# The recurrent mixer's projections spread one to a level over the first attention's last two levels and the second's first six, and the second attention's values behind them

## The reference

```python
p = (u @ w_in).astype(jnp.float32)
p_pool, p_hg, p_rw, p_gla = jnp.split(p, [G, 5 * G, 5 * G + RWKV_COLS], axis=-1)
...
prev = jnp.pad(p_rw, ((0, 0), (1, 0), (0, 0)))[:, :T]
p_rw = p_rw + (prev - p_rw) * rwkv_mu
rr, rk, rv, xw, xa, xg = jnp.split(p_rw, [...], axis=-1)
w_log = -jax.nn.softplus(-(rwkv_w0 + jnp.tanh(xw) @ rwkv_w2)) - 0.5
a = jax.nn.sigmoid(rwkv_a0 + xa @ rwkv_a2)
g_r = jax.nn.sigmoid(xg) @ rwkv_g2
kk = split_heads(rk * rwkv_k_k)
kk = kk / jnp.maximum(jnp.sqrt(jnp.sum(kk * kk, axis=-1, keepdims=True)), 1e-12)
rk = rk * (1.0 + (a - 1.0) * rwkv_k_a)
o_r = rwkv7_scan(r_h, split_heads(decay), k_h, v_h, kk, split_heads(a))
```

## Time and profile before

| | |
|---|---|
| median of 3 runs | 1793.57 us (1792.46 to 1795.89) |
| profiled execution, its own time | 1796.89 us |
| its span, first to last instruction | 1795.1 us |
| mean granted clock of TensorE | 0.969 |
| TensorE busy | 1722.1 us |
| VectorE busy | 875.8 us |
| ScalarE busy | 674.9 us |
| GpSimdE busy | 129.5 us |

### The profile page before, as it was taken

One profiled execution on the slowest core, in us unless ns is written; L12 is line 12 of the kernel. 1 busy time (PEld: TensorE's weight loads), 2 busy tenths in 40 slices (PEclk: granted clock), 3 DMA queues, 4 the chain that ended last, 5 costly groups with the idle time before them and its releaser, 6 DMA issues.

```text
span 1795.1 us, 22262 instructions
## 1 busy us (share of the span) xinstructions
PE 1722.1 (96%) x8752; PEld 1405.7 (78%) x8752; DVE 875.8 (49%) x1169; ACT 674.9 (38%) x1017; POOL 129.5 (7%) x126
## 2 busy tenths in 40 slices
PE   7999999999999899999999999969998899999997
PEld 6777778878778788888888777859986688888886
DVE  5633445532445565444334774665345654444333
ACT  5145664225555333332224443463132433333221
POOL 0001002001001000000004000001330200000000
PEclk9999999999999999999999999965999999999998
DMA  5322213322222133223333211100001222333331
GB/s 188 125 71 71 83 51 103 126 81 75 78 65 83 59 107 103 96 94 89 97 97 141 71 59 48 61 17 1 1 19 47 82 83 95 99 100 92 96 97 56
DMA packets 40744, 143.91 MB, mean 80 GB/s; under 512 B 4816, under 2 KB 4832, under 8 KB 40384
## 3 DMA queue, kind: packets, MB, share of 16 engines
q1 hardware_dynamic: 37008, 130.87, 22.6%
q0 software_dynamic: 2192, 8.73, 1.5%
q10 hardware_dynamic: 1440, 2.88, 0.4%
HBM read 140.37 MB, written 2.10 MB: 79 GB/s over the span
## 4 chain that ended last, share of the span: by engine, by line
PE 79%; DVE 13%; ACT 5%; issue 1%; ACTq 0%; DVEq 0%
PE bank L450 22%; PE bank L452 21%; PE bank L451 21%; PE bank L432 9%; DVE sb_w_low L1115 2%; DVE sb_E L1115 2%; PE bank L438 2%; DVE sb_near L1502 1%; PE bank L668 1%; PE bank L647 1%; ACT sb_E L1833 1%; PE bank L604 1%; ACT sb_w_high L1833 1%; DVE sb_xg_low L1123 1%; DVE sb_x L1115 1%
## 5 line engine op out<-in xcount | busy, mean ns | idle before, releaser
L1115 DVE TENSOR_TENSOR sb_w_low<-sb_raw,sb_w_high 128x1024 fp32r<-128x1024 f32 (+1 forms) x253 | 310.0, 1225 | 391.1 <-ACT sb_w_high L1833 385.2
L450 PE MATMUL bank<-sb_xg_high,sb_w_high 128*128 128x512 f32 x1176 | 469.2, 399 | 26.0 <-DVE sb_xg_low L1123 16.1
L452 PE MATMUL bank<-sb_xg_high,sb_w_low 128*128 128x512 f32 x1176 | 461.9, 393 | 0.0
L451 PE MATMUL bank<-sb_xg_low,sb_w_high 128*128 128x512 f32 x1176 | 461.7, 393 | 0.0
L1833 ACT ACTIVATE sb_w_high<-sb_raw 128x1024 fp32r<-128x1024 f32 (+1 forms) x253 | 263.2, 1040 | 357.1 <-PE bank L452 325.3
L450 PEld LDWEIGHTS bank<-sb_xg_high,sb_w_high 128*128 128x128 f32 x1176 | 223.0, 190 | 93.0 <-issue 33.3
L452 PEld LDWEIGHTS bank<-sb_xg_high,sb_w_low 128*128 128x128 f32 x1176 | 222.9, 190 | 47.8
L451 PEld LDWEIGHTS bank<-sb_xg_low,sb_w_high 128*128 128x128 f32 x1176 | 223.3, 190 | 44.7
L452 PE MATMUL bank<-sb_h_high,sb_w_low 128*128 128x512 f32 x352 | 136.9, 389 | 0.0
L450 PE MATMUL bank<-sb_h_high,sb_w_high 128*128 128x512 f32 x352 | 136.9, 389 | 0.0
L451 PE MATMUL bank<-sb_h_low,sb_w_high 128*128 128x512 f32 x352 | 136.9, 389 | 0.0
(11 more groups left out here) (334 smaller groups left out, 2123.4 us busy)
## 6 DMA issues: line engine op xcount, KB each, us to landing
sb_raw<-w_ffn_in SPq DMA_DIRECT2D x88, 512.0 KB, 3.3
sb_raw<-w_ffn_out SPq DMA_DIRECT2D x32, 512.0 KB, 3.6
sb_raw<-w_tok SPq DMA_DIRECT2D x24, 512.0 KB, 3.7
sb_raw<-w_mix_f SPq DMA_DIRECT2D x18, 512.0 KB, 3.2
sb_raw<-w_rot SPq DMA_DIRECT2D x16, 512.0 KB, 3.7
sb_raw<-w_qk SPq DMA_DIRECT2D x16, 512.0 KB, 3.3
sb_raw<-w_out SPq DMA_DIRECT2D x16, 512.0 KB, 3.2
sb_raw<-w_ffn_out SPq DMA_DIRECT2D x16, 384.0 KB, 3.1
```

Of the source, the lines that this page charges most:

```text
L450: e.matmul(out, w[0], v[0], start=first, stop=False)
L451: e.matmul(out, w[0], v[1], start=False, stop=False)
L452: return e.matmul(out, w[1], v[0], start=False, stop=last)
L1115: e.tensor_tensor(out, a, b, op).then_inc(*v.up(*signal))
```

## The change

The recurrent projections start in the first attention's levels 8 and 9, with the two that feed the decay and the gates (`RWKV_ORDER` begins with 6 and 7), and go on with one in each of the second's levels 0 to 5. The second attention's four value units fill its levels 6 to 9. The operand steps become functions of their own, called from the levels between which their inputs are ready. Several operands get buffers that others leave: projections go straight to `rE`, `kI`, `rv` and `gates_in` in place of `mixed`, the scan's sum and the decay are raised in place (`cum`, `sigma`), and the two gates (`gates_in`) and `shifted` lie where gla's values come later. The first half of the mixing waits for `far` of size 128 alone and for each token tile's values by itself. The SiLU of gla's gate moves from level 4 to the place behind the root in `finish_gla`.

```diff
+
+RWKV_ORDER = (6, 7, 2, 3, 0, 1, 4, 5)
...
     order += [t["w_mix_ga"]] + mixer_tiles(14, 16, 15, 17)
-    values, projections = mixer_group(1), mixer_tiles(*range(2, 10))
-    order += values[0:3] + [projections[0], values[3]] + projections[1:]
+    order += mixer_tiles(*(2 + f for f in RWKV_ORDER)) + mixer_group(1)
...
         r = region(first_at, second_at)
-        m.mixed = r.room("mixed", 8, SEQ)
-        m.shifted = r.room("shifted", 2, SEQ)
+        m.rE, m.kI, m.rv, m.bI = (r.room(n, 2, SEQ) for n in ("rE", "kI", "rv", "bI"))
+        m.sigma = r.room("sigma", 2, SEQ)
+        r = region(values_at, end)
+        m.gates_in, m.shifted = r.room("gates_in", 2, SEQ), r.room("shifted", 2, SEQ)
+        m.own = [room[:, f, :] for room in (m.rE, m.kI, m.rv, m.gates_in) for f in range(2)]
...
                 i = take(("mixed", name, half), ("mixed landed", name, half))
                 p.wait_ge(*of("near done", name))
-                p.wait_ge(*of("far", name, last, 3))
-                p.wait_ge(*of(landed("v", 3), name, 3))
+                p.wait_ge(*of("far", name, last - 1 + half, 3))
                 for t in (2 * half, 2 * half + 1):
+                    p.wait_ge(*of(landed("v", t), name, t))
                     for h in HEADS:
...
         def rwkv_steps():
-            for f in range(8):
+            for f in RWKV_ORDER:
                 projected("rwkv", f, "rwkv landed", f)
                 yield
...
+        projections = rwkv_steps()
+        values_h, others = token_major("v", "hgrn", 1, n), gla_steps()
+
+        def decay_and_gate_in():
...
+        def gate_out():
+            for half in range(2):
+                i = take(("gate out", half), ("g tok", half))
+                p.wait_ge(*of("rwkv sigmoid"))
...
+        def key_norm():
             i = take(("key norm",), ("key floored",))
             p.wait_ge(*of("key squares"))
...
+        def key_turned():
             for f in range(2):
                 i = take(("key turned", f), ("key scaled", f))
                 p.wait_ge(*of("key spread"))
...
+        def bonus_sums():
             i = take(("bonus",), ("bonus",))
             p.wait_ge(*of("rE"))
...
+        def fill_hgrn(n):
+            if n == 0:
+                next(values_h)
+                next(values_h)
+                pool_outputs()
+            else:
+                next(values_h if n < 3 else others if n < 8 else projections)
+            if n == 9:
+                decay_and_gate_in()
+
+        linear_attention("hgrn", fill_hgrn)
+        values_g = token_major("v", "gla", 1, n)
         def fill_gla(n):
-            if n < 2:
-                next(values_g)
-                next(projections)
-            elif n < 6:
-                next(projections)
-                if n in (2, 4):
-                    next(projections)
-                if n == 5:
-                    p.mark("xg read", MIX_NORM)
-            else:
-                next(operand_prep)
+            next(projections if n < 6 else values_g)
+            if n == 1:
+                gate_out()
+            if n == 3:
+                key_norm()
+            if n == 4:
+                key_turned()
+            if n == 9:
+                p.mark("xg read", MIX_NORM)
+                bonus_sums()
...
+            if n == 0:
+                finish_hgrn()
+            if n == 3:
+                key_floor()
+            next(projections if n < 6 else values_g)
+            if n == 1:
+                decay_sums()
+            if n == 5:
+                keys_scaled()
+            if n == 6:
+                keys()
+            if n == 7:
+                receptance()
+            if n == 8:
+                receptance_faded()
...
             fill(len(ORDER))
+            if name == "gla":
+                a.wait_ge(*of("bonus in"))
+                act(small[:, 112:128], bank("bonus")[:, 0:16], "bonus")
             for half in range(2):
...
+        def decay_in():
+            a.wait_ge(*of("rwkv mixed", 6))
+            act(m.gates_in[0:64, 0, :], m.gates_in[0:64, 0, :], "rwkv tanh", func=ACT.Tanh)
...
         def fill_hgrn(n):
+            if n == 9:
+                decay_in()
...
-            yield
+        values_g = value_steps("gla")
+
+        def gates():
+            a.wait_ge(*of("y made", "hgrn"))
...
+            a.wait_ge(*of("rwkv mixed", 7))
+            act(m.gates_in[:, 1, :], m.gates_in[:, 1, :], "rwkv sigmoid", func=ACT.Sigmoid)
+
+        def gate_out():
             for half in range(2):
                 a.wait_ge(*of("gate out", half))
...
-            yield
+
+        def key_squares():
+            a.wait_ge(*of("rwkv mixed", 3))
+            for f in range(2):
...
+        def decay_exps():
             a.wait_ge(*of("sigma before"))
             act(m.eB, m.cum, *STEP, func=ACT.Exp, scale=-HALF_E)
-            act(m.rE, m.cum, *STEP, func=ACT.Exp, scale=HALF_E)
-            act(m.tmp, m.tmp, "rwkv exps", func=ACT.Exp, scale=-HALF_E)
...
+        def key_spread():
+            a.wait_ge(*of("key inverse"))
+            act(heads(flat(mem.square)), small[:, 176:192].unsqueeze(2).to_broadcast([P, 16, 64]), "key spread")
...
+            if n == 0:
+                finish_hgrn()
+                gates()
+            if n == 2:
+                key_squares()
+                decay_exps()
             if n == 4:
-                bend_gate("gla")
+                key_spread()
+            next(projections if n < 6 else values_g)
+            if n == 1:
+                gate_out()
...
-        inverse(m, finish_gla)
+
+        def gla_out():
+            finish_gla()
+            bend_gate("gla")
+
+        inverse(m, gla_out)
```

191 lines of the change are left out of this document (69 added, 122 removed).

## The result

The changed kernel takes 1814.84 us, median of 4 runs (1813.39 to 1815.61), against 1794.32 for the kernel before on the same chip (4 runs, 1792.46 to 1795.89): a ratio of 1.0114, 95% interval 1.0096 to 1.0131. It is **slower by 20.5 us**. The profiled execution has a span of 1811.6 us against 1795.1, so 16.5 us of it can be followed in the two traces. (Four executions further down stand apart from the others of their kernel, at a lower mean clock: 1933.9 us in run 7, 2849.6 in run 12, 1808.4 and 1808.7 in run 10; the medians count them, the ratios do not.)

A forecast was written before the change was run, and what follows sets the result against it. A second-attention level with one projection was taken as bound by VectorE and ScalarE, not TensorE. +15.5 us up to the first product with Pm and +2 in the inverse gave +17.5, on the median 1811 us; 80% range 1794 to 1827.

The forecast's parts named there:

- the first product that reads Pm: Behind the second attention's Gram products, ahead of the inverse: comes at 1268.9 us against 1253.4, 15.5 us later.
- the inverse: Behind a gap of 2 to 3 us its clock may fall: 2 us in the sum, bounds 0 and 75.
- the last value unit: Made behind the second attention's last 256-wide products, ahead of the mixing: 7.4 us, between 5.7 and 11.4.
- VectorE's chain: Serial steps through the second attention's levels: 102.3 us from "y made", last factors ready at 1211.6 us against 1198.9.
- y made: VectorE finishes the first attention's output, where the second attention's chain starts: at 1109.3 us against 1110.1.
- last operand: The last VectorE step that the inverse needs ("rE"), 3.8 us behind the last factors: 1215.4 us against 1221.0.
- TensorE's wait at the turned keys: In filling 4 of the second attention: TensorE ends projection 4 near 1153 us and waits until 1164.5.
- The mixing falls to half after some 2 us and takes 15.5: Second attention's mixing, behind the two-column bonus sums: clock falls to half, from near 1225.5 us to 1241.
- Rival 2: Clock returns with the last value unit and holds through mixing and Gram products: 1796 to 1799 us; 25%.
- The Gram products at half, and the SiLU: From the mixing's end to the first product with Pm: 25.5 us at half clock plus 2.4 for the SiLU.
- rival 1: Half clock in mixing, Gram products and a good part of the inverse: some 1822 us, up to 1840; 22%.
- What follows the inverse is untouched: Stages behind the inverse to the end of the span: no change in time.

The follow-up runs named there:

- run 7: The changed kernel with bonus sums behind the inverse's last pass, early SiLU, early weight splits and projection 5 at level 4: 1796.53 us, ratio 1.0020 to the kernel before.
- run 12: The kernel before with only the loosened end (presets of X, output squares and sums, and root earlier): 1795.58 us, ratio 1.0004.
- run 10: As run 9, and projection 5 made at level 4, so no value unit is left behind the last factors: 1783.35 us, ratio 0.9935 to the kernel before.
- Run 1: The changed kernel with projection 5 one level earlier, at level 4 beside projection 4: 1807.85 us, ratio 1.0082 to the kernel before.
- run 4: The changed kernel with ScalarE's splits of the weight's high part ahead of sigmoids, squares and exponentials: 1814.57 us, ratio 1.0113 to the kernel before.
- run 2: The changed kernel with the two-column bonus sums behind the mixing instead of ahead of it: 1806.45 us, ratio 1.0067 to the kernel before.
- run 11: The changed kernel with only the bonus sums moved, into TensorE's wait ahead of the last 256-wide products: 1802.48 us, ratio 1.0048 to the kernel before.
- run 9: The changed kernel with early weight splits, bonus sums in the wait ahead of the 256-wide products, and presets, SiLU, squares and root earlier: 1783.06 us, ratio 0.9938.
- run 5: The changed kernel with bonus sums behind the inverse's last pass and the SiLU among the token copies: 1802.32 us, ratio 1.0044 to the kernel before.
- run 6: As run 5, with ScalarE's splits of the weight's high part early as well: 1793.24 us, ratio 1.0000 to the kernel before.
- Run 3: The changed kernel with the gate's SiLU among ScalarE's copies of the turned tokens: 1806.88 us, ratio 1.0076 to the kernel before.
- run 8: The kernel before with 24 more unused 128x512 products between its last 256-wide product and the second attention's mixing: 1792.82 us, ratio 0.9990.

## Why the prediction was right, point by point

It said 1811 us, 17.5 us more on the span; measured were 1814.8 and 16.5 on the profiled spans. Median and profiled execution part by the spread between executions: the profiled one was the fastest of its four runs. That the sum on the span came within 1 us is partly luck: the first product that reads Pm came 3.6 us sooner than forecast, and 1.1 us more in the inverse and 1.5 us behind it filled most of that again. The mechanism held; its largest miss is the last value unit.

- **VectorE's chain.** "y made" was said to come at 1109.3 and came at 1107.5; the whole of TensorE's timeline ahead of it is 1.3 us early. The chain of 102.3 us took 101.9, with last factors at 1209.4 (said: 1211.6) and the last operand at 1213.0 (said: 1215.4). Its waits for two weights, 5.1 and 4.8, were 4.99 and 4.85. Run 1 shows that the chain and not TensorE sets this end, run 4 that it moves with those splits. (Before, four of the second's levels carried two units, not three; the sum does not use it.)
- **TensorE's wait at the turned keys**, until 1164.5, ended at 1163.0 behind 9.71 us. Runs 1, 7 and 10 add what I had not priced: filling it lengthens the chain by 2.0 to 3.3 us and makes another wait, for the banks of the values.
- **The last value unit** was put at 7.4 us, between 5.7 and 11.4. It took 5.8, at full clock; the guess of a mixed clock was too slow by 1.6 us. So the mixing started at 1222.0 and not 1225.5; 1.3 of the 3.5 us are the early start.
- **The mixing falls to half after some 2 us and takes 15.5.** The spell began at 1224.0, 2 us into it, and it took 15.5. The reason given, the two-column sums ahead of it, was an inference from one place of the trace before; runs 2 and 11 show it: with the sums elsewhere the mixing takes 9.1 us, though in run 2 TensorE still pauses 0.8 us ahead of it. Rival 2's case, "the clock comes back with the last value unit", was right. "And holds" failed, in the mixing by the sums; behind a mixing at full clock the Gram products kept it to their end in runs 7 and 9 and lost it in runs 5, 6 and 11.
- **The Gram products at half, and the SiLU:** 25.5 + 2.4 = 27.9 us; measured 27.8. Run 3 takes 2.4 of it away with the SiLU.
- **The first product that reads Pm** was put 15.5 us later, and came 11.9 later: 1.6 for the value unit, 1.3 for the early start, the rest small terms.
- **The inverse** was put at +2 us (range 0 to 75), and took 3.1 more: 6.8 us at half behind the 2.70 us wait. Run 3 closes the wait and the fall goes; run 4 has the same wait (3.18 us) and loses 11 us against the kernel before. So rival 1, the long fall, was a real possibility, and that the fall here was short is luck.
- **"What follows the inverse is untouched":** it took 1.5 us more. Over the traces whose edits do not touch it (all but those of runs 5 to 7) it is anything from 466.0 to 468.8, so this is no more than the spread.

The term that the prediction had as one block, a mixing and Gram stage that ran at half before and would again, hid the most: it priced the change as a delay of 15.5 us behind that block, where the block itself could be had for 22.7 us (9.1 + 13.6, run 9) instead of 46.0 (17.3 + 28.7). In the changed kernel TensorE was busy for all of the 15.40 us of the mixing at a mean clock of 0.57, and from 1224.0 to 1261.0 for 37.0 of 37.0 us at 0.50. The Trainium skill ("TensorE: Matmul & The Clock Gate", Part 1) says that sustained matmul activity releases the throttle; this trace again does not agree.

What stays open: why the clock fell 8 us into the Gram products in runs 5, 6 and 11, at a wait of 1.52 us, and held through the same products with the same wait in run 7. Whether it is the two columns of the bonus sums that bring the fall, or any product at that place would, was not tried. And whether the 24 products of run 8 work by their width or by their place was not tried apart; run 7's mixing had full clock with none.

## What to carry to other kernels

Where TensorE's clock is half, price each move by the clock it leaves behind and not only by its length: here eight products of two columns ahead of a long narrow stretch cost 12 us, and 24 useless wide ones cost nothing. An edit that shortens the critical chain can measure as nothing because the clock takes it back further on (run 4) and be worth its full size once that is mended (run 6), so try it again after each mending. Spreading work evenly over levels is no gain where another engine's chain sets the level; look for what is then left standing alone behind the last one, and for small steps such as a table load that stood in slack before.

## What the runs showed of the hardware

- The same mixing (82 records of narrow products) took 17.3 us at granted clock 0.50 in the kernel before and 9.0 at 1.00 in run 8, which adds only the 24 products right ahead of it.
- Two-column sums begun at full clock were followed by a fall within about 2 us of their end in the changed kernel and in runs 1 to 4, 7 and 8; begun at half clock ahead of wide products (runs 9 and 11), they were not in the way of a rise behind them. In the kernel before the clock even rose during other two-column sums (from 1186.50 on, rise at 1187.0), to fall again 1.8 us behind them. In runs 5 and 6 the same sums at the inverse's end brought no fall.
- A fall at the start of the inverse lasted 6.8 us in one kernel and 24 us in another, behind waits of 2.70 and 3.18 us: the length of a spell is not to be read from the wait.
